# Reading the moving weight columns of the gate stage in another order

## The reference

```
h2 = rms_norm(x, mlp_norm[i])
x = x + jnp.square(jax.nn.relu(h2 @ w_ffn_up[i])) @ w_ffn_down[i]

gate = jax.nn.sigmoid(rms_norm(x, ple_norm[i]) @ w_ple_gate[i])
x = x + gate * (p[i] @ w_ple_proj[i])
```

## Time and profile before

| | |
|---|---|
| median of three runs | 2443.51 us (2441.5 to 2444.57) |
| span of the profiled execution, first to last instruction | 2440.9 us |
| what lies around the span | the page gives no time of its own for that execution; the median stands 2.6 us above the span |
| TensorE busy | 99% of the span |
| mean granted TensorE clock | 0.996 of full speed |
| gate stage on TensorE | about 1149.8 to 1255.8 us of the span |

### The profile page before, as it was taken

The page is one execution under the profiler, slowest core; times in us unless marked ns, Lnnn a source line. Parts: engine busy times, 40 slices in busy tenths (PEclk is TensorE's granted clock), DMA queues, the critical chain, the costliest instruction groups (busy, mean ns, idle before and its releaser), DMA issues.

```text
span 2440.9 us, 40493 instructions
## 1 busy us (share of the span) xinstructions
PE 2411.3 (99%) x18716; PEld 2210.0 (91%) x18716; DVE 1359.4 (56%) x1130; ACT 989.9 (41%) x936; POOL 192.0 (8%) x139
## 2 busy tenths in 40 slices
PE   8999999999999999999999999999999999999999
PEld 7999988998998998988789999877998999999897
DVE  5597666545444445455558567585554554555553
ACT  4643145443333333344453364265433333333332
POOL 0004120020120110120000002000000000000000
PEclk9999999999999999999999999999999999999999
DMA  7553046655656555665556644244554754755654
GB/s 222 169 156 88 21 156 226 194 185 205 186 194 199 183 206 187 193 226 188 180 153 193 191 139 141 76 155 144 179 190 156 241 185 163 231 182 178 215 160 138
DMA packets 334534, 425.44 MB, mean 174 GB/s; under 512 B 4186, under 2 KB 249358, under 8 KB 333982
## 3 DMA queue, kind: packets, MB, share of 16 engines
q1 hardware_dynamic: 333053, 418.55, 52.2%
q0 software_dynamic: 1136, 4.17, 0.5%
q10 hardware_dynamic: 176, 0.14, 0.0%
HBM read 420.75 MB, written 2.10 MB: 173 GB/s over the span
## 4 chain that ended last, share of the span: by engine, by line
PE 91%; DVE 5%; issue 2%; ACT 2%; DMA 0%; POOLq 0%; POOL 0%; DVEq 0%; ACTq 0%
PE PS L621 81%; PE PS L820 2%; PE PS L711 1%; DVE ring_r L1925 1%; PE PS L657 1%; PE PS L994 1%; PE PS L1274 0%; DVE ring_r L2195 0%; PE PS L1178 0%; ACT arena_r L1348 0%; PE PS L878 0%; PE PS L933 0%; PE PS L1102 0%; PE PS L925 0%; DMA arena<-in_attn_norm 0%
## 5 line engine op out<-in xcount | busy, mean ns | idle before, releaser
L621 PE MATMUL PS<-arena_r,arena_r 128*128 128x256 f32 (+1 forms) x6944 | 1544.1, 300 | 3.7 <-DVE ring_r L2195 1.4
L621 PEld LDWEIGHTS PS<-arena_r,arena_r 128*128 128x128 f32 x6944 | 1123.4, 188 | 60.3 <-issue 4.3
L1883 DVE TENSOR_TENSOR ring_r<-ring,arena_r 128x2048 fp32r<-128x2048 f32 x316 | 730.5, 2316 | 658.8 <-ACT arena_r L1348 658.8
L1348 ACT ACTIVATE arena_r<-ring 128x2048 fp32r<-128x2048 f32 (+1 forms) x394 | 691.6, 1761 | 976.2 <-PE PS L621 971.4
L621 PE MATMUL PS<-arena_r,ring_r 128*128 128x256 f32 x3072 | 852.2, 277 | 0.0
L621 PEld LDWEIGHTS PS<-arena_r,ring_r 128*128 128x128 f32 x3072 | 578.7, 188 | 0.0
L621 PE MATMUL PS<-ring_r,arena_r 128*128 128x512 f32 (+1 forms) x1504 | 539.0, 372 | 0.0
L621 PE MATMUL PS<-arena_r,actT_r 128*128 128x512 f32 (+1 forms) x1184 | 454.3, 384 | 0.0
L621 PEld LDWEIGHTS PS<-ring_r,arena_r 128*128 128x128 f32 x1504 | 275.9, 188 | 49.7 <-issue 1.4
L621 PEld LDWEIGHTS PS<-arena_r,actT_r 128*128 128x128 f32 x1184 | 222.3, 188 | 44.6
L621 PE MATMUL PS<-actT_r,arena_r 128*128 128x256 f32 (+1 forms) x656 | 184.5, 281 | 0.0
(11 more groups left out here) (336 smaller groups left out, 1443.5 us busy)
## 6 DMA issues: line engine op xcount, KB each, us to landing
ring<-in_w_ffn_up SPq DMA_DIRECT2D x32, 2048.0 KB, 9.3
ring<-in_w_ffn_down SPq DMA_DIRECT2D x32, 2048.0 KB, 8.0
ring<-in_w_in SPq DMA_DIRECT2D x22, 2048.0 KB, 8.0
ring<-in_w_gate SPq DMA_DIRECT2D x22, 2048.0 KB, 8.1
ring<-in_w_up SPq DMA_DIRECT2D x22, 2048.0 KB, 8.1
ring<-in_w_in SPq DMA_DIRECT2D x32, 1024.0 KB, 5.3
ring<-in_w_out SPq DMA_DIRECT2D x16, 2048.0 KB, 8.2
ring<-in_w_down SPq DMA_DIRECT2D x12, 2048.0 KB, 8.0
```

What stands on the lines that cost most here:

```text
L621: mm = pe.matmul(dst, r32(w, early), r32(x, early), start=first and q == 0, stop=last and q == 2)
L1348: return act.activation(dst, src, ACT.Copy, scale=scale)
L1883: v.tensor_tensor(r32(u), u, high_of(high_home(n, i, j)), ALU.subtract).then_inc(S["w_low"], counts(units, j))
```

## The change

Three of the four units read the same 512 moving words in another order. Unit 0 reads all even columns and then all odd ones (step two). Unit 1 takes a word of the first half and a word of the second half in turn (columns 0, 256, 1, 257 and so on). Unit 2 reads pieces of 16 neighbouring words, the even pieces first and then the odd ones. Unit 3 is left as it was. Both parts of the weights, high and low, are read in the unit's order.

The output columns come to stand in PSUM in the order in which they were read. The sigmoid on ScalarE puts them back: it reads the PSUM bank from one end to the other (`GATE_SUMS` undoes `GATE_ORDER`) and writes to `gate_sb` in the unit's order. What VectorE reads after that is laid out as before.

No instruction is added, removed or moved on any engine. On TensorE and VectorE every instruction has the shape that it had. On ScalarE the six sigmoid instructions of units 0, 1 and 2 are written as 128x2x256, 128x256x2 and 128x2x16x16 in place of 128x512.

```diff
@@ -353,6 +353,11 @@
+    GATE_ORDER = (lambda a: a.rearrange("p (i w) -> p w i", w=2), lambda a: a.rearrange("p (w i) -> p i w", w=2),
+                  lambda a: a.rearrange("p (b w i) -> p w b i", w=2, i=16), lambda a: a)
+    GATE_SUMS = (lambda a: a.rearrange("p (w i) -> p w i", w=2), lambda a: a.rearrange("p (i w) -> p i w", w=2),
+                 lambda a: a.rearrange("p (w b i) -> p w b i", w=2, i=16), lambda a: a)
...
-        def split_tokens(n, out, xh, xl, i=None, per=2, units=UNITS[4], ready=None, after=None):
+        def split_tokens(n, out, xh, xl, i=None, per=2, units=UNITS[4], ready=None, after=None, order=lambda a: a):
...
-                        mm = three(out[:, t, :], (xh(x)[:, tok], xl(x)[:, tok]), (wh[:, k, :], wl[:, k, :]),
+                        mm = three(out[:, t, :], (xh(x)[:, tok], xl(x)[:, tok]), (order(wh[:, k, :]), order(wl[:, k, :])),
...
-            split_tokens(N_GATE + c, pair[c % 2], lambda k: gh[:, k, :], lambda k: gl[:, k, :],
+            split_tokens(N_GATE + c, pair[c % 2], lambda k: gh[:, k, :], lambda k: gl[:, k, :], order=GATE_ORDER[c],
...
-                ins = act.activation(gate_sb[:, t], pair[c % 2][:, t], ACT.Sigmoid, scale=rs_gate[:, t:t + 1])
+                ins = act.activation(GATE_ORDER[c](gate_sb[:, t]), GATE_SUMS[c](pair[c % 2][:, t]), ACT.Sigmoid,
+                                     scale=rs_gate[:, t:t + 1])
```

## The result

The changed kernel takes 2467.75 us (median of four runs, 2464.62 to 2468.42) against 2444.04 us for the kernel before beside it (four runs, 2441.5 to 2445.7). The ratio is 1.0095, with a 95% interval of 1.0082 to 1.0109. The profiled execution is the one of 2464.62 us; its span is 2462.8 us, 21.9 us longer than before, and 1.8 us lie around it.

What follows compares the result with a forecast made beforehand. TensorE was taken to bound the kernel, busy 99% of the span. Units 0, 1, 2 and the sigmoids summed as 0 + 20.5 + 0 + 0 = 20.5 us, so 2443.5 + 20.5 = 2464.0 us, range 2442 to 2470 us.

Steps and rivals of the forecast that it cites:

- The bound and the pace: Gate stage: TensorE's chain is unbroken, so MATMUL delays reach the end; 231.1 ns a MATMUL, 213.3 at a word a clock.
- Unit 0, taken at 0: Unit 0's 96 MATMULs: step two costs nothing; the other end, one more clock a word, is 20.5 us.
- the flat rows of VectorE: VectorE's line 2264 takes 685 to 693 ns for 512 words in runs of 32 down to 1, with step two.
- the reasoning on neighbours: TensorE's supply fetches neighbouring words together; unit 1 takes the neighbours from every fetch, unit 0 leaves some.
- Unit 1, taken at 20.5 us: Unit 1's 96 MATMULs: halves in turn need two clocks a word, 19.0 to 22.2 us, 20.5 us in the middle.
- The second rival: Step two costs as well: units 0 and 1 both need two clocks a word, 2484.5 us; chance 0.11.
- Below nothing: Gain if all of the 17.8 ns went from 288 MATMULs: 5.1 us, giving 2438.4 us.
- the fixed part: The 17.8 ns of a gate MATMUL's 231.1 ns beyond the 213.3 ns of 512 columns at one a clock.
- Unit 2, taken at 0 with 2.5 us above: Unit 2's 96 MATMULs: pieces of 16 cost nothing; at most two clocks for each of 31 jumps, 2.5 us.
- Sigmoids: ScalarE's sigmoids of units 0 to 2: taken at 0; at half the writing pace 0.87 us more a unit, still covered.
- The 2.6 us: Whole kernel: the median lies 2.6 us above the span of the profiled execution.
- The rule on lines: SBUF is read in 16-byte lines, two accesses in a row per line: step two and pieces free, halves slow.

Runs made afterwards that it cites:

- experiment 7: Against the changed kernel, new orders in units 0 to 3: two streams with step two; 0, 2, 1, 3; two streams with step four; two streams of pairs. 2466.51 us.
- experiment 3: Against the changed kernel, all four units read two halves in turn, unit 1's order; 2440.26 us against 2443.37 for the kernel before, ratio 0.9983.
- experiment 11: Against the changed kernel, only unit 0 keeps its new order, step two, and units 1 to 3 read as stored; 2468.13 us, ratio 1.0098.

## Why the prediction was right in time and wrong in cause

The forecast was 2464.0 us in a range of 2442 to 2470; 2467.75 was measured. The sum of the stage was 20.5 us; the trace has 20.6. That agreement is an accident, because the two terms behind it were exchanged.

- **The bound and the pace.** Right. TensorE is the chain, nothing else in the stage sets the end, and the 20.6 us of the stage went to the end of the traced execution (21.9 us with what lies around the stage). Two clocks a word as the price of a slow read (one doubled read, not four) was right as well: 452.5 ns against my 429 to 462.
- **Unit 0, taken at 0.** This step failed: it measured +21.3 us. I had put the other end at 20.5 us, and had let the flat rows of VectorE and the reasoning on neighbours decide for 0. I had said that VectorE's pace does not reach TensorE's, and then took its answer all the same.
- **Unit 1, taken at 20.5 us.** This step failed too: -1.5 us. "The halves take the neighbours away from every fetch" was the wrong picture. What fits most of the orders measured is not which words follow one another in the whole stream but which follow at its even places and which at its odd ones (theory R, experiment 7). The second rival, that step two costs as well, had its half right and held on to the same picture for unit 1.
- **Below nothing.** The end below nothing was priced for all 17.8 ns of the fixed part, 5.1 us over three units, and 15.3 ns of the 17.8 went in unit 1. I wrote that nothing in the rows says that it goes. The rows did show that this part was no constant, 226.9 and 231.1 ns.
- **Unit 2, taken at 0 with 2.5 us above.** +0.9 us, inside.
- **Sigmoids.** Covered, as forecast; unit 1's pair took 0.87 us more, the figure worked out for half the pace of writing.
- **What lies around the span.** The 2.6 us were the median less the span of another execution. In the traced run of the changed kernel it is 1.8 us.
- **The rule on lines.** The Trainium skill, "Advanced Engine Details and Errata", section "SBUF Cachelines", asks for at least two hits on a line of 16 bytes. Step two has two hits on each line and takes twice the time here (452.5 ns for 231.1). With two halves in turn no two words that follow one another lie in one line, and that is the fastest order (215.8 ns). The measurements decide against the rule as I applied it to TensorE's moving read.

The medians lie 23.7 us apart, 3 us more than the stage explains. The traced execution was the fastest of the four; the other three took 2467.57 to 2468.42 us. The traces show where such differences can come from. The stretch from the end of the second block's first projection to the start of its output projection is the same work in the kernel before, in the full change, in experiment 3 and in experiment 11, in this order. The columns are the stretch, its length, the busy us (and instructions) of PE, PEld, DVE, ACT and POOL, the granted clock, the DMA share and GB/s:

```profile
1422.54:1661.44 238.90, 231.16 (x1657) 199.73 (x1657) 165.40 (x232) 114.46 (x205) 18.73 (x14) 0.97 0.38 125
1443.80:1683.37 239.57, 233.87 (x1658) 201.30 (x1657) 165.79 (x232) 114.55 (x205) 18.79 (x14) 0.96 0.38 124
1416.18:1660.07 243.89, 236.03 (x1657) 203.85 (x1657) 165.99 (x232) 114.78 (x205) 18.77 (x14) 0.95 0.37 122
1443.86:1687.49 243.63, 235.81 (x1658) 203.49 (x1657) 166.03 (x232) 114.71 (x205) 18.76 (x14) 0.95 0.38 122
```

VectorE and ScalarE are busy for the same time within 0.6 us in all four. TensorE is busy 2.7 to 4.9 us longer where the granted clock is lower, and the stretch takes up to 5.0 us more. That is the 5.0 us that experiment 3 lost again. It is also why the span of experiment 11 is 26.0 us longer than before: 21.3 us in the gate stage and 4.7 us here. One piece of the stretch shows it closely, first in the full change and then in experiment 11:

```profile
1633.80:1643.00 9.20, 9.15 (x55) 7.72 (x55) 7.08 (x18) 8.51 (x41) 0.00 (x0) 1.00 0.20 73
```

```profile
1634.80:1647.10 12.30, 12.28 (x57) 10.27 (x55) 7.10 (x17) 9.86 (x42) 0.00 (x0) 0.72 0.15 55
```

The granted clock is 1.00 in the one and 0.72 on average in the other, so part of it stood at the lower level. TensorE also stands idle in this stretch, 5.7 us of it in the full change and 7.7 to 7.9 us in the others. The mean clocks of the single runs fit: the other three runs of the changed kernel have 0.994 where the traced one has 0.995, and in experiment 3 the two runs at 0.996 took 2435.3 and 2437.38 us, the eight at 0.994 or 0.995 2438.63 to 2443.0 us. That this is what lengthened the other three runs was not shown, since they have no trace, and why the clock falls in one execution and not in another is open.

## What to carry to other kernels

When TensorE streams close to one fp32r word a clock, the order of the moving words is a cost of its own, and the same words can take 216, 231 or 452 ns for 512. Other types were not tested. Reading two contiguous streams in turn was the fast order here, faster than reading from end to end. It can be put back for nothing where the result is read from PSUM with step two, or where the next MATMUL loads it as its stationary operand with step two. The flat rows of a slower engine did not carry over to TensorE, and a number that comes out right is no proof of its terms: only the groups of one unit each in the chain told them apart.

## What the runs showed of the hardware

All distances are from one 512-column fp32r MATMUL to the next, at a granted clock of 1.00 (2.4 GHz, 213.3 ns at a word a clock).

| order of the moving words | ns | words in a row from one line of four, for each reader |
|---|---|---|
| two streams in turn, 4 to 256 words apart | 215.8 | 4 |
| as stored | 231.1 | 2 |
| 0, 2, 1, 3, 4, 6, 5, 7 | 231 | 2 |
| two streams in turn, each with step two | 231.1 | 2 |
| two streams in turn, each of pairs at a distance of four | 231 | 2 |
| step 2, 3, 4, 16 | 452, 451, 460, 433 | 1 |
| pairs of neighbours at a distance of four | 452 | 1 |
| two streams in turn, each with step four | 452 | 1 |
| pieces of 16, even ones first | 240.0 | 2, a jump every 16 words |
| two halves in turn, pieces of four words | 255.4 | 2, a jump every four words |
| two halves in turn, pieces of two words | 327.8 | 1, back and forth |
| four quarters in turn | 280.0 | 1, back and forth |
| eight eighths in turn | 487.5 | 1, back and forth |

Theory R orders the first eight rows without an exception, and two of its numbers (units 0 and 3 of experiment 7) were told ahead against a rival that gave others: two readers share the stream, one with the even places and one with the odd ones, and each needs at least two words in a row from one line. The readers themselves are an inference; no trace shows them. That a line holds four words fits the runs: with eight, step two would still give each reader two words in a row and the time of the order as stored; with two, the order as stored would itself be slow. Theory R does not give the whole time. Pieces of 16 and of four words should run like the order as stored, and take 8.9 and 24.3 ns more, some 0.3 and 0.2 ns for each of their 31 and 127 jumps. It does not explain either why step 16 takes 433 ns and step four 460, or why MATMULs of the stage before took 226.9 ns in the order as stored. The last three rows suggest that a return to a line left shortly before is cheaper than a new one (280 and 328 against 452 ns), as long as there are few; how many lines a reader holds was not measured, nor why eighths cost more than step four.

PSUM took the sums in pieces of two words, in two halves, at no cost (231 ns). ScalarE wrote SBUF with step two at its usual pace and with two streams in turn about 1.7 times slower (2.14 for 1.27 us). VectorE and ScalarE read PSUM with step two at no cost (746 for 747 ns, 1.27 us). The stationary load with step two took 196 for 188 ns.
